# Crossed quarters in a scan's inverse, and a projection streamed over four banks with the attention dealt out beside it

## What is computed

```python
def hybrid_mixer(h_lat, h_ctx, ...):
    p_lat = h_lat @ w_in                     # (256, 3328)
    p_ctx = h_ctx @ w_in                     # (256, 3328)
    rc = rwkv_prepare(p_ctx[..., :1792], ...)   # token shift, mixing with mu, gates, unit keys
    rl = rwkv_prepare(p_lat[..., :1792], ...)
    yc, sf, sb = wkv_bidir(rc, (zero, zero))    # scans forwards and backwards
    yl, _, _ = wkv_bidir(rl, (sf, sb))
    a_lat = rwkv_output(yl, rl, ...)
    # q, k, v: 512 columns each, from p[..., 1792:]
    o_l = diff_attn_latent(rope_2d(ql), ql, rope_2d(kl), kc, concat(vl, vc), lam)
    out_lat = concat(a_lat, subln(o_l)) @ w_out   # the context's output likewise
```

## Time and profile before

| what | us |
|---|---|
| median of 3 runs | 3557.92 |
| lowest, highest | 3556.57, 3561.64 |
| the profiled execution | 3568.06 |
| its span | 3566.3 |
| PE busy | 3255.4 (91%) |
| DVE busy | 1893.3 (53%) |
| ACT busy | 1406.6 (39%) |
| POOL busy | 354.1 (10%) |

### The profile page before, as it was taken

The page is one execution under the profiler, slowest core; times in us unless marked ns, Lnnn a source line. Parts: engine busy times, 40 slices in busy tenths (PEclk is TensorE's granted clock), DMA queues, the critical chain, the costliest instruction groups (busy, mean ns, idle before and its releaser), DMA issues.

```text
span 3566.3 us, 54709 instructions
## 1 busy us (share of the span) xinstructions
PE 3255.4 (91%) x22888; PEld 2800.9 (79%) x22888; DVE 1893.3 (53%) x2581; ACT 1406.6 (39%) x2039; POOL 354.1 (10%) x387
## 2 busy tenths in 40 slices
PE   8999999999999999999898689897999979896897
PEld 7877887897987788789685578786788868786795
DVE  4456645445445664544524766654333367676554
ACT  4355444435444544443521433322323244412443
POOL 2000000100100000010101243321000001033000
PEclk9999999999999999999999889898999999987999
DMA  9755656675765565575440000002232223500454
GB/s 274 221 158 171 185 152 202 197 228 181 234 206 154 153 199 151 182 227 160 146 132 12 1 8 2 2 2 95 77 96 94 78 78 88 142 1 12 142 177 135
DMA packets 449228, 459.78 MB, mean 129 GB/s; under 512 B 18288, under 2 KB 347184, under 8 KB 449008
## 3 DMA queue, kind: packets, MB, share of 16 engines
q1 hardware_dynamic: 428624, 385.08, 36.6%
q0 software_dynamic: 20384, 71.52, 6.0%
HBM read 455.50 MB, written 1.05 MB: 128 GB/s over the span
## 4 chain that ended last, share of the span: by engine, by line
PE 75%; DVE 14%; ACT 5%; issue 3%; DMA 2%; POOL 0%; DVEq 0%; SPq 0%; ACTq 0%; POOLq 0%
PE banks L312 20%; PE banks L313 20%; PE banks L314 20%; DVE weights_lo L298 1%; DMA raw_weights<-in_w_ffn_gu 1%; PE banks L4352 1%; PE banks L3595 1%; PE banks L3597 1%; PE banks L3576 1%; ACT weights_hi L290 1%; PE banks L1291 1%; PE banks L1902 1%; PE banks L1932 1%; DVE arena L3998 1%; DVE first_input_split L1302 1%
## 5 line engine op out<-in xcount | busy, mean ns | idle before, releaser
L298 DVE TENSOR_TENSOR weights_lo<-raw_weights,weights_hi 128x1024 fp32r<-128x1024 f32 (+2 forms) x399 | 472.9, 1186 | 505.8 <-ACT weights_hi L290 429.5
L290 ACT ACTIVATE weights_hi<-raw_weights 128x1024 fp32r<-128x1024 f32 (+2 forms) x399 | 409.6, 1028 | 610.3 <-PE banks L314 562.0
L263 DVE TENSOR_TENSOR weights_lo<-raw_weights,weights_hi 128x1024 fp32r<-128x1024 f32 x180 | 223.1, 1241 | 471.0 <-ACT weights_hi L256 281.9
L256 ACT ACTIVATE weights_hi<-raw_weights 128x1024 fp32r<-128x1024 f32 x180 | 190.6, 1060 | 515.4 <-PE banks L314 510.2
L312 PE MATMUL banks<-first_input_split,weights_hi 128*128 128x256 f32 (+1 forms) x1218 | 354.6, 291 | 13.6 <-DVE weights_lo L298 6.8
L314 PE MATMUL banks<-first_input_split,weights_lo 128*128 128x256 f32 (+1 forms) x1218 | 348.4, 286 | 0.0
L313 PE MATMUL banks<-first_input_split,weights_hi 128*128 128x256 f32 (+1 forms) x1218 | 347.1, 285 | 0.0
L298 DVE TENSOR_TENSOR third_weights_split<-raw_weights,third_weights_split 128x1024 fp32r<-128x1024 f32 (+1 forms) x173 | 207.2, 1197 | 199.9 <-ACT third_weights_split L290 156.0
L312 PE MATMUL banks<-work_split,weights_hi 128*128 128x512 f32 (+2 forms) x776 | 272.4, 351 | 18.9 <-DVEq L2459 15.0
L290 ACT ACTIVATE third_weights_split<-raw_weights 128x1024 fp32r<-128x1024 f32 (+1 forms) x173 | 178.9, 1034 | 248.8 <-PE banks L314 225.9
L313 PE MATMUL banks<-input_split,weights_hi 128*128 128x512 f32 (+2 forms) x776 | 270.7, 349 | 0.0
(11 more groups left out here) (598 smaller groups left out, 7190.4 us busy)
## 6 DMA issues: line engine op xcount, KB each, us to landing
raw_weights<-in_w_ffn_gu SPq DMA_DIRECT2D x176, 512.0 KB, 4.9
raw_weights<-in_w_in SPq DMA_DIRECT2D x144, 512.0 KB, 3.6
raw_weights<-in_mlp_w SPq DMA_DIRECT2D x128, 512.0 KB, 3.9
arena<-in_ada_w POOLq DMA_DIRECT2D x96, 512.0 KB, 6.2
raw_weights<-in_w_ffn_down SPq DMA_DIRECT2D x80, 512.0 KB, 3.4
raw_weights<-in_w_branch SPq DMA_DIRECT2D x48, 512.0 KB, 3.6
raw_weights<-in_ssd_w_in SPq DMA_DIRECT2D x48, 512.0 KB, 3.9
raw_weights<-in_w_mkv SPq DMA_DIRECT2D x32, 512.0 KB, 4.2
```

Source lines behind the costliest of these rows:

```text
L256: last = s.activation(self.w_hi[:, u % 2, :], self.raw[:, u, :], ACT.Copy)
L263: last = v.tensor_tensor(self.w_lo[:, u % 2, :], self.raw[:, u, :], self.w_hi[:, u % 2, :].bitcast(F32), ALU.subtract)
L290: last = s.activation(hi, raw, ACT.Copy)
L298: last = v.tensor_tensor(lo, raw, hi.bitcast(F32), ALU.subtract)
```

## The change

**The projection** is now written out by a class `HybridInput`. Its chunks come in another order: k, q and v of the attention first, then the narrow chunk `low`, then k, r and v of the scan. It uses banks 0 to 3 only: a chunk's tile t may enter bank t when ACT, which now does all the emptying, has taken the chunk before from it. After each tile of each unit (six products) the generator yields.

**The attention** takes its steps at these yields. The generator `beside` begins when two chunks (k and q) are out, and takes one step of each chain, at every second yield two. The rounds wait for the third chunk (v). The buffers moved to the work area. `mixed_tokens` begins only when the projection has ended.

**The scan.** The first pair and `outputs` now begin when attention and mixing have both ended, the second pair 25 ticks later.

**The inverse.** The inverse itself is kept in the other half of the partitions than its transpose. Step 1 of a level writes from half b to half 1 - b, and in step 3 the two products of a block stand next to each other, both with rows 1 - b, one with columns b, the other with columns 1 - b. The first transposes write both inverses.

```diff
+class HybridInput:
+        self.chunks = [(q + RW, RW), (q, RW), (q + 2 * RW, RW), (low, SEQ), (r + RW, RW), (r, RW), (r + 2 * RW, RW)]
...
+    def values(self):
+        return 3 * ROWS if self.taken >= 3 * ROWS else 0
...
+            s.activation(self.rows[:, t, at:at + width], c.ps[:, t, 0:width],
+                         ACT.Copy).then_inc(c.projection_taken, 1)
...
+        for chunk, (_, width) in enumerate(self.chunks):
+            for u in range(UNITS):
+                n = chunk * UNITS + u
+                self.split_ahead(n + 2)
...
+                for t in range(ROWS):
...
+                        if t == 0:
+                            pe.wait_ge(c.lo_made, first + n + 1 + UNITS)
...
+                        if u == 0 and chunk > 0:
+                            pe.wait_ge(c.projection_taken, (chunk - 1) * ROWS + t + 1)
+                        for j in range(per_unit):
+                            k = u * per_unit + j
+                            last = c.three_products(pe, c.ps[:, t, 0:width], x_hi[:, k, tokens], x_lo[:, k, tokens],
+                                                    hi[:, j, :], lo[:, j, :], k == 0, k == KD - 1)
...
+                    if u == UNITS - 1:
+                        self.take(chunk, t)
+                    yield
...
-    c.gemm_token_major(range(ROWS), 6, column_chunks(a["hy_w_in_2"][0], 0), BANK,
-                       *token_copies(c, rows, range(ROWS)), more=True, tiles_made=c.tiles_made)
-    n = HYB - 6 * BANK
-    c.gemm_token_major(range(ROWS), 1, column_chunks(a["hy_w_in_2"][0], 6 * BANK, n), n,
-                       *token_copies(c, rows[:, :, 6 * BANK:], range(ROWS), n))
-    c.loaded()
+    def beside():
+        while projection.taken < 2 * ROWS:
+            yield
+        c.loaded()
...
+        for n in itertools.count():
+            for s in attention * (1 + n % 2):
+                if s in attention and next(s, True):
+                    attention.remove(s)
+            yield
+    both = beside()
+    for _ in projection.run():
+        next(both)
...
             for b, h in blocks:
-                last = pe.matmul(g.of_block(b, h, P), block(g.inv, b, h), blockwise[b * HD:(b + 1) * HD, 8, :],
-                                 start=True, stop=True)
+                one = blockwise[b * HD:(b + 1) * HD, 8, :]
+                pe.matmul(block(g.sums(0), b, h), block(g.inv, b, h), one, start=True, stop=True)
+                last = pe.matmul(block(g.sums(1), 1 - b, h), one, block(g.inv, b, h), start=True, stop=True)
...
                 for b, h in blocks:
-                    last = pe.matmul(g.of_block(b, h, 256), block(g.level, b, h), block(g.inv_t, b, h), start=True,
-                                     stop=True)
+                    last = pe.matmul(g.of_block(1 - b, h, 256), block(g.level, b, h), block(g.inv_t, b, h),
+                                     start=True, stop=True)
...
                 for b, h in blocks:
-                    pe.matmul(g.of_block(b, h, P), block(g.inv, b, h), block(g.half, b, h), start=True, stop=True)
-                for b, h in blocks:
-                    last = pe.matmul(g.of_block(b, h, 0), block(g.half, b, h), block(g.inv, b, h), start=True,
-                                     stop=True)
+                    inv, half = block(g.inv, 1 - b, h), block(g.half, 1 - b, h)
+                    pe.matmul(block(g.sums(0), b, h), inv, half, start=True, stop=True)
+                    last = pe.matmul(block(g.sums(1), 1 - b, h), half, inv, start=True, stop=True)
...
-    after, ticks, late = None, 0, False
-    while running:
+    begun, ticks = None, 0
+    while running or begun is None or ticks <= begun + STAGGER:
...
-                if s is pre:
-                    running += [scan(g, chain_ends([mixing])) for g in groups[0:2]]
-                    after = ticks
-                if s in attention and not any(x in running for x in attention):
-                    running.append(outputs())
-                    late = True
         ticks += 1
-        if late and after is not None and ticks >= after + STAGGER:
+        if begun is None and not running:
+            begun = ticks
+            running = [scan(g, chain_ends([mixing] + attend)) for g in groups[0:2]] + [outputs()]
+        if begun is not None and ticks == begun + STAGGER:
             running += [scan(g, chain_ends([mixing] + attend)) for g in groups[2:4]]
-            late = False
```

132 lines of the change are left out of this document (101 added, 31 removed).

## The result

The changed kernel takes 3581.19 us (median of five runs, 3577.05 to 3584.40) against 3557.92 (five runs, 3556.57 to 3564.69). The ratio is 1.006, with a 95% interval of 1.0043 to 1.0077. Forecast was 3535, a gain of 23 us; it became a loss of 23. The profiled execution took 3584.4 us (span 3582.6, mean granted clock 0.939) against 3568.06 before (0.944), so in the profiles the sum should have given 3545 and is 39 off.

What follows compares the result with a forecast made beforehand. PE, busy 91% of the span, was taken as the bound, full in projection and scan but with room in the mixing. Terms +55 - 12 - 66 = -23 us gave a median of 3535; range 3500 to 3565, leaving out 2 in 10.

Steps and rivals of the forecast that it cites:

- Part 1: Projection with the attention beside it: 145 us becomes 200, +55, from 34 us more PE work and 21 of waits.
- Part 2: Mixing stage without the attention: 68 us instead of 79.7, -12, with 60 and 76 as ends.
- Part 3: Scan with the second pair 25 steps behind, products unchanged: 393 us instead of 424.9, -32, at 93.3 a shared chunk.
- the lag evens PE out: Scan rival, 22%: at half a chunk of lag a chunk costs 76 us instead of 84, 27 us more gain, 3508.
- Part 4: Inverse levels in the scan: two crossed sets take 0.47 us instead of 0.93, 37 us of PE time; scan 359.
- the forecast is wrong if PE's saving fell into waits: Sign of error in the scan: a chunk stays at 93 us though the quarters overlap, PE's saving lost waiting for DVE.
- starves: Projection rival, 18%: late softmax holds the products behind it, deciding from 44 us of waits instead of 21; at 60, 3574.
- quarters do not overlap: Rival on the inverse's crossed products, 8%: the 37 us stay, about 32 of them on the path, 3567.

Runs made afterwards that it cites:

- the move alone: The changed kernel with the inverse's two product loops put back as before, so without crossed quarters: 3605.05 us, ratio 1.0132 of the kernel before.
- double issue: Each level's crossed products issued twice: in the kernel before with crossed quarters 3606.52 us, ratio 1.0105; in the changed kernel 3613.91 us, ratio 1.0155.

## Why the prediction was wrong, step by step

*Part 1, right.* +55 forecast, +52.6 measured. PE's own work for the attention was 38.4 us (181.35 - 142.93) instead of 34 (a round's terms add up to 5.2 us, of which the forecast took 4.9), the waits 16 instead of 21. 9.6 of the waits stand before the softmax's transposes, with 2.6 us at the longest, where up to 6 had been allowed for a round in the narrow chunk.

*Part 2, right.* 70.7 instead of 68. PE stood still 10.2 us before the second sequence and its first products there took 1.86 us, as in rows 4; the stretch before the unit keys was 12.5.

*Part 3, the step that failed.* The forecast took 93.3 us for a shared chunk from three windows of the kernel before, in which the pairs' chunks begin 20 us apart, and used it for pairs that begin 37 to 57 us apart. That price belongs to that position. With the new one PE waits 24.3 us for DVE at the transposition before the Grams (29.9 with POOL; 13.6 before), and the scan is 422.6 instead of 393. Of these 30 us some 12 are the clock (123 us at half clock instead of 99), and 18 are the position. That the lag is the cause and not the move of the attention is shown by the lag of 37, which brings the first pair's next chunk back to 24 to 29 us behind the second pair's, the wait to 5.7 us and the scan to 400.8. In the terms of part 3 a lag of 37 has three levels of 3.0 us more alone at each end: 45 us, then 139 steps or 3.16 chunks at 93.3, and 46, which is 386 us; 14 more for 127 us at half clock make 400. At this position the old price holds. The text named this danger in the reverse sense only: the rival "the lag evens PE out" had half a chunk of lag as a gain of 27 us, with "a lockstep order pays each engine's lateness to all four" as the doubt. The doubt was the effect. A transposition that waits for DVE holds the ready products of the other pair behind it, so two unlike stretches side by side do not even out.

*Part 4, right in kind, a third of it missing.* Four quarters do overlap, at the 0.47 us that was worked out. (One of its two reasons was read too kindly: L3707's sixteen records fit in 0.61 us, not in the 0.47 of a set on two quarters.) PE's busy time in the scan fell by 34.1 us (362.3 to 328.2), near the forecast 37. The scan fell by 22.4 instead of 34, or by 28 with the half clock taken out (361 to 333). 12 us came back as idle time with a lag of 25, 19 with 37 (where 10 are waits for instructions) and 16 in the order of before (13 of them for instructions). The line "the forecast is wrong if PE's saving fell into waits" named what to look for; it half happened. A level of a pair is a chain PE, ACT, PE, DVE, so with less PE work in it the wait for the sum grows: L3697 for L3727 10.4 us after, 6.2 without crossing.

*The clock, not in the sum.* The forecast took the clock as it was, and named a lower one only as a sign of being wrong. The mean is 0.9460 before, 0.9425 with the move alone and 0.9395 in the change, and the whole step costs 17 us. The windows place it in the scan: 135 us at half clock instead of 99, of which 24 come with the move alone (123) and 12 with the crossing. That is 18 us if PE works in that time, and it lies inside the 30 and the 11 that parts 3 and 4 missed (12 and 6).

What lowers the clock is not shown. Missing PE work seemed to be it in the order of before, where crossing took the mean from 0.946 to 0.940 and double issue gave 0.9457 again. In the changed order it does not hold: double issue gave 0.9408 against 0.9395, the move alone with a lag of 37 had all its PE work and 0.9378, and a lag of 44 did the work of the change at 0.927. Products in the mixing's pauses raised the clock there and saved nothing. So each order of the instructions came out with its own mean clock, and no run tells why.

*The sum.* +55 - 12 - 32 - 34 = -23 was forecast. By the profiles it was +52.6 - 9.0 - 2.3 - 22.4 = +18.9. Of the 41 us that the scan is over its forecast, some 18 are the position of the pairs, 18 the clock and 6 the part of the crossing that became waits (an estimate, by the last column of the balance). The rivals "starves" and "quarters do not overlap" gave nearly the measured time, 3574 and 3567, for reasons that are refuted: neither the wait of 44 us nor 0.93 us for two sets is there.

What stays open: why one kernel's runs differ in clock by up to 0.010 (3549 to 3585 us for the crossed quarters alone), why the orders differ in clock, and by what rule PE outruns the supply of its instructions. That the waits called issue are that supply rests on the packets' times in 58 waits of three traces and on the doubling, which raises them from 14 to 39 us; no run changed the supply alone. None of the kernels beats the kernel before beyond the measurement; crossed quarters in its own order come out at 1.0003 and 1.0017.

## What to carry to other kernels

The price of a stage in which two chains interlock belongs to their relative position: before moving one chain, look for the wait that would stand in the in-order queue before the other's ready work, and scan the lag as a number of its own (here 25, 37 and 44 gave scans of 400, 385 and 447 us, the last by its clock). Before a parameter's effect is read from a run, see in the trace that it moved an instruction: a lag of 37 in the order of before moved none. Work taken from the busiest engine in a chain of short steps pays in part, here 14, 14 and 30 us of some 34 by the position of the pairs; the rest becomes waits. Where runs of one kernel scatter, set time against granted clock first: it showed a saving of 14 us that the clock had hidden.

## What the runs showed of the hardware

- Products of 64 x 64 on all four quarters of the array run at 32 records in 0.46 us, twice the rate of two quarters, although neighbours share their rows.
- At this rate PE stops with nothing to wait for, 14 us in a scan in fourteen waits of 0.25 to 1.6 us, and each time goes on 1.25 to 1.58 us after a 16 KB packet of the instruction queue. With the same number of instructions at half the rate it does so for 0.9 us.
- One program's executions differ in the mean granted clock, and the time with it: 3547 us at 0.945 and 3585 at 0.935, with 102 and 172 us at half clock in the scan and PE idle for 74 and 75. A kernel of 91% busy PE loses 2.4 to 3.3 us of 3560 for each 0.001.
- Kernels with equal PE work in another order have another mean clock: 0.9395, 0.9385 and 0.9268 with lags of 25, 37 and 44.
